# A slot without scores in a hybrid decoder step, and one turning of scores moved by a step

## What is computed

```python
def project_in(x, pos, ln_w, w_in, w_gla_a2, b_gla_a):
    h = rms_norm(x, ln_w)
    proj = jnp.einsum('bsd,de->bse', h, w_in)
    ...
    gate_pre = (jnp.einsum('bsr,rk->bsk', glr, w_gla_a2) + b_gla_a).astype(jnp.float32)
    log_a = (jax.nn.log_sigmoid(gate_pre) / GLA_TAU).reshape(B, S, GLA_HEADS, GLA_DK)

def dilated_window_attn_prompt(q, k, v, window, dilation):
    ...
    s = jnp.einsum('bnqhd,bnkhd->bnhqk', qb, kk).astype(jnp.float32)
    s = jnp.where(mask[None, :, None], s, -jnp.inf)
    m = jnp.max(s, axis=-1, keepdims=True)
    p = jnp.exp(s - m)
    den = jnp.sum(p, axis=-1, keepdims=True)
    o = jnp.einsum('bnhqk,bnkhd->bnqhd', p / den, vv.astype(jnp.float32))
```

## Time and profile before

| what | us |
|---|---|
| median of three runs | 2485.26 (2484.94 to 2485.51) |
| the profiled execution | 2486.58 |
| its span in the profile | 2484.8 |
| PE busy | 2450.7 |
| DVE busy | 1214.5 |
| ACT busy | 908.1 |
| POOL busy | 199.1 |

### The profile page before, as it was taken

The page is one execution under the profiler, slowest core; times in us unless marked ns, Lnnn a source line. Parts: engine busy times, 40 slices in busy tenths (PEclk is TensorE's granted clock), DMA queues, the critical chain, the costliest instruction groups (busy, mean ns, idle before and its releaser), DMA issues.

```text
span 2484.8 us, 37018 instructions
## 1 busy us (share of the span) xinstructions
PE 2450.7 (99%) x13710; PEld 1969.5 (79%) x13710; DVE 1214.5 (49%) x2860; ACT 908.1 (37%) x2163; POOL 199.1 (8%) x367
## 2 busy tenths in 40 slices
PE   9999999999999999999999999999999998999998
PEld 6888887887778888887888888788778755888887
DVE  5323422333321115565666666556756447656663
ACT  5224534443332214223544544445424233212221
POOL 0000000000000000112111111222222100000000
PEclk9999999999999999999999999999999999999999
DMA  6333323332323223457667666797777799444341
GB/s 192 103 121 114 105 91 125 103 100 90 112 96 102 93 91 117 144 170 240 209 220 224 202 204 204 215 296 216 206 230 215 219 338 346 172 161 151 140 167 68
DMA packets 209122, 416.97 MB, mean 168 GB/s; under 512 B 32513, under 2 KB 53521, under 8 KB 206833
## 3 DMA queue, kind: packets, MB, share of 16 engines
q1 hardware_dynamic: 166912, 293.60, 35.5%
q0 software_dynamic: 29712, 95.06, 13.1%
q10 hardware_dynamic: 12320, 25.96, 2.8%
HBM read 313.33 MB, written 112.99 MB: 172 GB/s over the span
## 4 chain that ended last, share of the span: by engine, by line
PE 93%; DMA 3%; DVE 2%; ACT 1%; issue 1%; SPq 0%; POOL 0%; DVEq 0%; ACTq 0%
PE b_acc L1231 20%; PE b_acc L1233 19%; PE b_acc L1232 19%; PE c_p_s L1281 3%; PE c_p_o L1304 3%; PE c_p_t L1292 3%; PE c_p_qk L1268 3%; PE f_p_b L2002 2%; PE f_p_b L2004 2%; PE f_p_b L2003 2%; PE f_p_z L2002 2%; PE f_p_z L2004 2%; PE f_p_z L2003 2%; PE b_acc L1237 2%; PE b_acc L1238 1%; PE e_p_o L1923 1%
## 5 line engine op out<-in xcount | busy, mean ns | idle before, releaser
L1231 PE MATMUL b_acc<-b_whi,hT_hi 128*128 128x512 f32 x2048 | 819.9, 400 | 3.9 <-DVE b_wlo L967 1.5
L1233 PE MATMUL b_acc<-b_whi,hT_lo 128*128 128x512 f32 x2048 | 799.5, 390 | 0.0
L1232 PE MATMUL b_acc<-b_wlo,hT_hi 128*128 128x512 f32 x2048 | 798.6, 390 | 0.0
L1231 PEld LDWEIGHTS b_acc<-b_whi,hT_hi 128*128 128x128 f32 x2048 | 384.4, 188 | 101.2 <-issue 9.8
L1233 PEld LDWEIGHTS b_acc<-b_whi,hT_lo 128*128 128x128 f32 x2048 | 384.5, 188 | 82.4
L1232 PEld LDWEIGHTS b_acc<-b_wlo,hT_hi 128*128 128x128 f32 x2048 | 385.1, 188 | 73.4
L967 DVE SCALAR_TENSOR_TENSOR b_wlo<-b_raw,a_lnw,b_whi 128x512 fp32r<-128x512 f32 x268 | 192.7, 748 | 365.3 <-ACT b_whi L759 364.9
L773 ACT COPY b_stage<-b_acc 128x512 f32<-128x512 f32 (+2 forms) x198 | 115.3, 582 | 539.6 <-PE b_acc L1233 529.4
L797 ACT ACTIVATE c_sm<-c_sm,c_ends 128x256 f32<-128x256 f32 (+1 forms) x384 | 172.8, 451 | 129.9 <-DVE c_ends L1052 129.8
L759 ACT ACTIVATE b_whi<-b_raw,a_lnw 128x512 fp32r<-128x512 f32 x268 | 182.9, 714 | 3.9 <-ACT c_og L815 1.4
L771 ACT ACTIVATE b_stage<-b_acc 128x512 f32<-128x512 f32 x96 | 57.4, 598 | 307.7 <-PE b_acc L1233 307.3
(11 more groups left out here) (320 smaller groups left out, 3091.2 us busy)
## 6 DMA issues: line engine op xcount, KB each, us to landing
b_raw<-in_w_in SPq DMA_DIRECT2D x134, 512.0 KB, 4.3
tm<-b_stage SPq DMA_DIRECT2D x256, 256.0 KB, 2.1
a_x<-tm POOLq DMA_DIRECT2D x192, 256.0 KB, 4.9
b_ck<-in_cache_kv_w POOLq DMA_DIRECT2D x104, 256.0 KB, 5.0
c_qk<-tm SPq DMA_DIRECT2D x101, 256.0 KB, 3.6
f_m<-tm SPq DMA_DIRECT2D x16, 1024.0 KB, 5.8
c_v<-tm SPq DMA_DIRECT2D x53, 256.0 KB, 4.3
og<-c_og ACTq DMA_DIRECT2D x48, 264.0 KB, 3.9
```

The lines of the kernel that those rows point to most:

```text
L1231: nc.tensor.matmul(out, stat_hi, mov_hi, start=(k == 0), stop=False)
L1232: nc.tensor.matmul(out, stat_hi, mov_lo, start=False, stop=False)
L1233: return nc.tensor.matmul(out, stat_lo, mov_hi, start=False, stop=(k == KC - 1))
```

## The change

`plan_attention` takes the slot of the sample rows of chunk GLR, which is slot 65. A pair of units that would have its scores in the first step of that slot, step 130, gets the step after the next, and all later pairs of half 0 follow it: 22 units of tasks 10 to 15 move by two steps. What hangs on a pair's step moves with it: the turning of probabilities, the sums, the turning of keys, queries and outputs, and the loads of queries, keys and values that SP issues for tasks 12 to 15. Step 130 keeps the turning of (task 10, first pair)'s probabilities and the sums of (task 9, second pair), and turns the keys of task 11 instead of its queries; step 131 turns the output of task 9 as before. The last scores of half 0 are in step 152 instead of 150, and the last output is turned in step 157 instead of 155. Half 1 and the recurrence keep their steps.

In the tail PE's `turn_scores(1)` goes from tail step 4 to tail step 5, behind `turn_p(0)`.

```diff
--- before.py
+++ after.py
@@ -154,7 +154,7 @@
 Unit = namedtuple("Unit", "u i c q")
 
 
-def plan_attention(begin):
+def plan_attention(begin, short):
 
 
 
@@ -185,6 +185,8 @@
         start = {(0, 1): 33, (0, 0): 60, (1, 2): begin + 29, (1, 1): begin + 53, (1, 0): begin + 77}[x.half, x.g]
         at = max(at, 2 * start)
         for c in range(4):
+            if at == 2 * short:
+                at += 2
             units.append(Unit(len(units), i, c, at))
             at += 2 * (c % 2)
     return tasks, units
@@ -262,7 +264,7 @@
     item_at = [begin + 3 + m * (NSLOT - 6 - begin - 3) // N_IT for m in range(N_IT)]
 
 
-    tasks, units = plan_attention(begin)
+    tasks, units = plan_attention(begin, next(x.s for x in slots if x.chunk == GLR and x.kind == "new"))
     N_U = len(units)
     pairs = list(zip(units[0::2], units[1::2]))
     score_at = {xs[0].q: xs for xs in pairs}
@@ -2059,10 +2061,9 @@
                 over.recurrence_over(pe, 1)
                 new_scores()
                 turn_scores(0)
-            if q == 4:
-                turn_scores(1)
             if q == 5:
                 turn_p(0)
+                turn_scores(1)
             if q == 9:
                 turn_p(1)
```

## The result

| | before | after |
|---|---|---|
| median of 20 runs | 2483.85 (2481.36 to 2486.06) | 2488.03 (2483.27 to 2492.15) |
| mean and standard deviation of the 20 | 2483.88, 1.5 | 2487.75, 2.7 |
| profiled execution | 2486.58, span 2484.8 | 2486.11, span 2484.3 |

The ratio is 1.0015 [1.0008, 1.0021]: within 0.2%, slower by 3.9 us in the mean where +0.75 was forecast. The two profiled executions alone say the opposite, −0.5 us; that of before, 2486.58, lies above all of its twenty runs. Where the 3.9 us come from is what the experiments had to find.

A forecast was written before the change was run, and what follows sets the result against it. PE, busy 99% of the span, was taken as the bound. Slot 65 -4.25, handover +4.6 and tail +0.4 sum to +0.75 us on the median 2485.26: 2486.0 us, 8-in-10 range 2481.2 to 2489.8.

The forecast's parts named there:

- rival 3: Slot 65's clock falls anyway, only 1.55 us of idle is gained: +3.45 us, 2488.7 us; chance 0.15.
- Slot 65, idle time: PE's 2.53 us wait behind line 815 shrinks to about 1.0 us of idle; gain 1.55 us.
- Slot 65, clock: Half clock from 434.60 to about 440.0 would vanish: 2.7 us gained, bounds 0 and 2.7.
- The handover, idle time: Before gates(0) in slot 79, PE would wait 2.9 us for late-issued loads where it waited for none.
- Rival 2: Loads at slot 78 not late, only slot 65 and the tail count: -3.85 us, 2481.4 us; chance 0.10.
- Rival 4: Handover: store takes 3.6 us, PE waits 4.5, clock falls there and in tail: +5.05 us, 2490.3; chance 0.07.
- The handover, clock: Behind the wait before gates(0), a short clock fall was taken: 1.7 us lost, bounds 0 and 2.7.
- The tail: Slot 290: one 2.9 us wait instead of 2.25 and 0.2: +0.4 us, 0 to 1.7 more if the clock falls.
- Slots 66 to 78: Same insertions in other steps: late turning, two more table loads and moved loads cost nothing.
- rival 5: Table loads make ACT late in slot 76, PE's turning waits up to 2.6 us: 2488.6 us; chance 0.03.

The follow-up runs named there:

- gates_earlier: Kernel before with the recurrence of half 0 begun one slot earlier (gates(0) in step 157); 1.0073, median 2500.70 us.
- loads_late: Kernel before with the constants and rank columns of half 0 issued by SP one slot later; 1.0039, median 2491.94 us.
- tail_only: Kernel before with only the second pair's scores turned one tail step later; 1.0003, median 2486.26 us.
- after_again: The changed kernel measured and profiled once more, nothing altered; 1.0014 against before, median 2486.35 us.
- plan_only: The changed kernel with the tail of before, so only the skipped step 130; 1.0005 against before, median 2487.34 us.
- plan_again: plan_only measured once more, beside gate_filled on the same chip; 1.0009 against before, median 2486.11 us.
- gate_filled: plan_only with 12 idle products (2.7 us) in the gap ahead of gates(0); 1.0009 against before, median 2485.37 us.
- gates_later: plan_only with the recurrence of half 0 begun one slot later (gates(0) in step 161); 0.9991 against before, median 2482.03 us.
- both_filled: The changed kernel with 12 idle products in each new gap, before gates(0) and in tail step 5; 1.0014 against before, median 2486.92 us.
- start_early: plan_only with the window of 128 begun one slot earlier (59 for 60), last output in step 155; 0.9986 against before, median 2480.95 us.
- start_again: start_early measured once more to confirm it; 0.9988 against before, median 2480.71 us.
- slot_filled: Kernel before with 10 idle products (2.3 us) in the slot 65 gap ahead of step 132; 0.9993, median 2482.07 us.

## Why the prediction was right, and where its sum was off

The time was forecast within 0.2% and came out within it, +3.9 us against +0.75. The idle times were right nearly to the tenth; two terms of the clock were not, both to the same side, and the measured sum lies nearer to rival 3's +3.45 than to the forecast. That 2488.03 still lies inside the range is in part luck: the range was put on a median of three runs that lay 1.4 us above that of twenty. Point by point:

**Slot 65, idle time: right.** 0.95 us are left of 2.53, 1.0 was reckoned. Net of the scores that come later, 1.6 us are gained.

**Slot 65, clock: the step that failed in size.** The sum took 2.7 us as gained because the one execution in the earlier trace rows ran at 0.50 from 434.6 to 440. Four profiled executions have this gap: the fall cost 2.7 us in before, 1.7 in gates_earlier, 1.5 in loads_late and nothing in tail_only, 1.5 on average, and filling the gap gained 1.7 ± 0.5 over 11 runs. And the new slot 65 is not free of it: of seven profiled executions with the skipped step and the old start, five kept 1.00 (after, after_again, plan_only, plan_again, gate_filled) and two fell for 3.4 us (gates_later, both_filled), 0.5 on average. The gain is about 1.0 us, not 2.7. Rival 3, which had the clock fall anyway, is right in two executions of seven, and its number came near the measured one by other terms than its own.

**The handover, idle time: right.** 2.94 us against 2.9, and each link of the chain within 0.2 us. Rival 2 falls: the loads are late in every kernel that ends the attention one slot later without moving the gates. Rival 4's slow store falls too: moved by a slot, the last store landed after 2.0 or 2.1 us in all seven profiled executions that have it there. At its old place, with a 512 KB weight load issued 2.1 us ahead of it and still in flight, it took 3.6 in before, 3.4 in start_early, 3.6 in start_again and loads_late and 3.8 in tail_only, but 2.1 in slot_filled. In gates_earlier, where no weight load was in flight, it took 2.2. So all long landings have the load beside them, but it does not always bring one. The row decided here against the Trainium skill's formula ("DMA: Bandwidth & Descriptors", "Anatomy of one DMA"), by which the wait was estimated at 3.5 us. That it is paid is seen from two sides: gates_later, which keeps the later end and lacks this wait and what the clock does behind it, is 4.0 us below plan_only beside it, and loads_late pays for its wait in full.

**The handover, clock: right on average, wrong in kind.** 1.7 us had been taken as a short fall that always comes. The profiles show 3.1 us in after_again and plan_again and nothing in after and plan_only: 1.6 on average over four executions. (gates_earlier, with a wait of the same 2.9 us, lost 3.4.)

**The tail: the second term mis-sized.** +0.4 us was taken, with a fall of the clock as an addition. The 0.4 itself is right: from the mask's landing to the first product of slot 291 it is 6.7 us in before (1980.6 to 1987.32) and 7.15 in after and after_again (1978.4 to 1985.55). The waits were 2.82, 2.01 and 0.81 us, following the landing of the mask at 6.9, 6.1 and 4.9 us after its issue, and the clock fell for 3.4 us in after and in tail_only and not in after_again: two of three, about 1.7 us each. With 0.4 that makes +1.5 us; measured alone it was +0.9 ± 0.6. The 0 to 1.7 us of clock had been named as bounds and left out of the sum.

**Slots 66 to 78: right.** No PE wait stands there. The two further table loads come as reckoned and are hidden, so rival 5 falls; here too the activation follows within 0.1 us (520.43 and 524.27 in after's timeline).

**The sum again.** −1.6 (idle) − 1.0 (clock) + 2.9 + 1.6 (handover) + 1.5 (tail) = +3.4 us, against +3.9 and +3.5 in two measurements. The same terms give +1.9 for plan_only (measured 1.8 and 2.5). For start_early the 2.53 us and the 1.5 us of clock both go, −4.0 (measured −3.8 and −3.3). For gates_later they give −2.6, and with 1.1 us of its new waits −1.5 (measured −2.2). The terms are mean values from four, seven, four and three profiled executions, so each is uncertain by half a microsecond or more; that they fit is support, not proof. The larger spread of after (2.7 us against 1.5) is what falls that come by chance in two more places would make, but no run isolates it.

**What stays open.** What decides whether the clock falls in a given execution. What the fall at the handover costs on average, beyond the four profiles (plan_again against gate_filled is unresolved). And both_filled does not say whether anything is left in after when its gaps are filled, since its own filler cost time in the tail.

## What to carry to other kernels

An insertion skipped at one place makes all that follows end later, so look first at the fixed consumer behind the end: here buffers handed from one phase to the next over a store's landing, eight issues in a row and a load's landing, 9 us with only 6 us of work to cover them. Give the skipped slot back by starting earlier, not by ending later: here a start of 59 in place of 60 turned +2.2 us into −3.5 (means of two measurements each). And a clock fall seen in one profile is a chance and not a price; take more executions before it enters a sum at full size, and look whether a later wait hides it (below).

## What the runs showed of the hardware that was not expected

**Gaps of one length with and without a clock fall.** After 2.53 us of idle three executions of four fell, after 2.8 to 2.9 at the handover three of five (gates_earlier among them), each time from 1.00 to 0.50, for 3.4 or 6.8 us. Two executions fell in a slot with only 0.95 us of idle in two pieces around products of 32 columns. In the tail before did not fall after 2.25 us of idle between full slots, and tail_only fell after 2.01, so the length of the gap alone does not order them. With the gap filled there was no fall in slot_filled's slot 66 nor behind gates(0) in gate_filled and both_filled (1.00 each); these are three executions, too few to show that filling prevents it. The same program fell in one execution and not in the next (after and after_again, plan_only and plan_again). The Trainium skill ("TensorE: Matmul & The Clock Gate", "Part 1: The HAM clock gate") ties the clock to how busy the engine has been recently, and says of the slow start of a kernel that it differs from run to run. These traces agree: the falls named here all stand behind idle time of PE, and the chance shows in the middle of a program too.

**Landing times that vary between executions.** The sample's mask landed 4.8 to 7.1 us after its issue in these kernels, with the same transfers issued around it, and moves the tail's wait by 2 us. With such terms two profiled executions can't be subtracted from each other at the level of a few microseconds: here they said −0.5 us where 20 runs each said +3.9.

**A clock fall that costs nothing.** Late in the program, in a part that no kernel here touches, PE's wait for `f_bT_lo` goes from 1.9 us in before to 4.8 in start_again, which is the faster kernel all the same. PE's timelines there, of before and of start_again:

```profile
2069.19 1.09 PE L1923 MATMUL e_p_o<-e_vc_a,e_pm 128*64 128x512 f32 x1 [3.19 <-DMA b_raw<-in_cache_kv_w]
...
2077.70 0.50 PE L2002 MATMUL f_p_b<-w_wb_hi,f_bT_hi 128*128 128x512 f32 x1 [1.95 <-DVE f_bT_lo L2551]
```

```profile
2062.40 0.61 PE L1925 MATMUL e_p_o<-e_vc_a,e_pm 128*64 128x512 f32 x1 [3.21 <-DMA b_raw<-in_cache_kv_w]
...
2070.90 0.80 PE L2004 MATMUL f_p_b<-w_wb_hi,f_bT_hi 128*128 128x512 f32 x1 [4.84 <-DVE f_bT_lo L2553]
```

From the first line to the second it is 8.51 us in before, whose products ran at half clock (1.09 us each), and 8.50 in start_again, whose products ran at full clock (0.61 us each). In all fourteen profiled executions it is 8.48 to 8.52 us, while the wait at its end is anything from 1.9 to 4.9. PE works more slowly or waits longer for DVE, and the stretch takes as long. A fall of the clock, like a wait, costs time only where nothing behind it waits for something else.
